# Gated linear attention by pairs of chunks on one Trainium2 core, with ScalarE's Silu on the gate

## What is computed

```python
proj = h @ w_in                       # qa ka va | qb kb vb rb | zb
log_a = log_sigmoid(zb @ w_alpha + b_alpha) / 16
def step(state, (qn, kn, vn, an)):    # four chunks of 64 frames, four heads
    cum = cumsum(an); total = cum[-1]
    k_dec = kn * exp(total - cum)
    state = exp(total) * state + k_dec^T @ vn      # (128, 256) for each head
    return state, qn @ state
ob = rms_norm(o, g_norm_b) * silu(rb)
y = concat([oa, ob]) @ w_out          # then norm, residual, router, experts
```

## Time and profile before

| | us |
|---|---|
| median of 3 runs | 1503.46 |
| lowest and highest | 1501.86, 1504.16 |
| span of the profiled execution, first to last instruction | 1501.0 |

### The profile page before, as it was taken

The page is one execution under the profiler, slowest core; times in us unless marked ns, Lnnn a source line. Parts: engine busy times, 40 slices in busy tenths (PEclk is TensorE's granted clock), DMA queues, the critical chain, the costliest instruction groups (busy, mean ns, idle before and its releaser), DMA issues.

```text
span 1501.0 us, 19016 instructions
## 1 busy us (share of the span) xinstructions
PE 1246.9 (83%) x7349; PEld 552.2 (37%) x7350; DVE 772.2 (51%) x1102; ACT 207.4 (14%) x477; POOL 45.4 (3%) x68
## 2 busy tenths in 40 slices
PE   4699999999999999976777767766776679999977
PEld 4588544744444443322222212212221223333322
DVE  5876257777688666534233323432342334555525
ACT  3011131221111032100000000000000001111103
POOL 0001200000000001000000000000000000000010
PEclk9899999999999999999789898988898989999989
DMA  9999979888789779999999999999999999999996
GB/s 354 393 383 385 368 261 361 307 337 304 295 321 382 306 292 395 427 423 426 428 426 424 428 426 425 425 429 426 425 427 427 426 425 428 426 426 425 427 426 262
DMA packets 101668, 581.93 MB, mean 388 GB/s; under 512 B 6680, under 2 KB 31536, under 8 KB 57856
## 3 DMA queue, kind: packets, MB, share of 16 engines
q1 hardware_dynamic: 98752, 572.81, 93.8%
q10 hardware_dynamic: 1664, 6.46, 1.1%
q0 software_dynamic: 1216, 2.17, 0.5%
HBM read 579.29 MB, written 2.13 MB: 387 GB/s over the span
## 4 chain that ended last, share of the span: by engine, by line
PE 38%; DMA 35%; SPq 16%; DVE 9%; issue 1%; ACT 1%; POOL 0%; ACTq 0%; DVEq 0%
DMA stream<-in_w 32%; PE ps L709 10%; PE ps L918 6%; PE ps L634 5%; SPq L546 5%; SPq L565 4%; SPq L540 4%; PE ps L972 3%; PE ps L791 3%; DMA stream<-in_w_ada 2%; DVE wk L1058 2%; PE ps L879 2%; PE ps L706 1%; PE ps L824 1%; PE ps L925 1%
## 5 line engine op out<-in xcount | busy, mean ns | idle before, releaser
L918 PE MATMUL ps<-stream,wk 128*32 128x512 f32 x2304 | 320.2, 683 | 135.7 <-DMA stream<-in_w 134.9
L1385 DVE TENSOR_TENSOR acc<-ps,acc 128x2048 f32<-128x2048 f32 x37 | 84.8, 2292 | 429.6 <-PE ps L879 429.6
L918 PEld LDWEIGHTS ps<-stream,wk 128*32 128x32 f32 x2304 | 70.6, 117 | 374.4 <-issue 296.6
L972 PE MATMUL ps<-stream,cst 128*32 128x512 f32 x1152 | 153.1, 660 | 61.8 <-DMA stream<-in_w 61.7
L709 PE MATMUL ps<-stream 128*128 128x512 f32 x448 | 199.2, 599 | 0.3 <-PE ps L634 0.3
L709 PEld LDWEIGHTS ps<-stream 128*128 128x128 f32 x448 | 83.9, 191 | 100.3 <-issue 99.6
L634 PE MATMUL ps<-stream 128*128 128x256 f32 x512 | 118.0, 394 | 1.8 <-ACT stream L1530 1.8
L634 PEld LDWEIGHTS ps<-stream 128*128 128x128 f32 x512 | 100.9, 198 | 16.7 <-issue 1.9
L925 PEld LDWEIGHTS ps<-cst,wk 128*128 128x128 f32 x576 | 70.2, 192 | 62.8 <-issue 62.8
L1058 DVE SCALAR_TENSOR_TENSOR wk<-stream,cc,wk 128x768 f32<-128x768 f32 (+1 forms) x90 | 83.6, 929 | 11.5 <-DMA stream<-in_w_ada 8.9
L879 PE MATMUL ps<-wk,cst 32*128 32x512 f32 x592 | 88.3, 668 | 0.8 <-ACT wk L1701 0.8
(11 more groups left out here) (275 smaller groups left out, 1015.5 us busy)
## 6 DMA issues: line engine op xcount, KB each, us to landing
stream<-in_w SPq DMA_DIRECT2D x190, 2048.0 KB, 40.8
stream<-in_w_ada SPq DMA_DIRECT2D x64, 1024.0 KB, 6.0
stream<-in_w_in SPq DMA_DIRECT2D x8, 4096.0 KB, 16.7
stream<-in_w_ada SPq DMA_DIRECT2D x64, 384.0 KB, 10.0
stream<-in_w_out SPq DMA_DIRECT2D x4, 4096.0 KB, 15.3
stream<-in_w_ada SPq DMA_DIRECT2D x16, 512.0 KB, 10.2
stream<-in_w_in SPq DMA_DIRECT2D x4, 2048.0 KB, 13.7
stream<-in_w_in SPq DMA_DIRECT2D x2, 3072.0 KB, 16.2
```

The costliest lines, as they stand in the source:

```text
L918: last = nc.tensor.matmul(bank(1 + m)[32 * g:32 * g + 32, :], xe[:, k + g, :], w13[m][:, k + g, :], start=(k == 0), stop=(k == KD - 4))
L972: last = nc.tensor.matmul(bank(2)[32 * g:32 * g + 32, :], hid[:, k, :], w2v[:, k, 512 * g:512 * g + 512], start=(k == 0), stop=(k == 3))
L1385: V.tensor_tensor(y4, ps[:, b0:b0 + 4, :], y4, ALU.add).then_inc(ysum_sb, 1)
```

## The change

Chunks are worked in pairs. `kv` t now makes both chunks of tile t, head by head: chunk 2t from partitions 0 to 63 and chunk 2t+1 from partitions 64 to 127, into different pairs of banks (`kv_of`). DVE works out both states, in two buffers. `glao` t multiplies both chunks, head by head, into the two halves of the output partitions. `silu` items are gone on both engines: ACT evacuates the blocks of the gate with Silu instead of Copy. The second state buffer takes the place of `la`, which nothing reads any more by then.

```diff
-    for j in range(5):
-        if j:
-            beside[25 + j].append(("glao", j - 1))
-        if j < 4:
-            beside[25 + j].append(("kv", j))
-    beside[26] += [("silu", 0, 0)]
-    beside[28] += [("gsq", 0), ("silu", 1, 0)]
-    beside[29] += [("gmul", 0, 0)]
-    beside[30] += [("gsq", 1), ("silu", 0, 1), ("gmul", 0, 1)]
-    beside[31] += [("gmul", 1, 0), ("glaT", 0)]
+    beside[25].append(("kv", 0))
+    beside[26] += [("glao", 0), ("kv", 1)]
+    beside[27] += [("glao", 1), ("gsq", 0)]
+    beside[28] += [("gsq", 1)]
+    beside[29] += [("gmul", 0, 0), ("gmul", 1, 0)]
+    beside[30] += [("gmul", 0, 1)]
+    beside[31] += [("glaT", 0)]
...
-            out += [("silu", 1, 1), ("gmul", 1, 1), ("partial", 4), ("wout", 0, 0), ("glaT", 1), ("mod", 4)]
+            out += [("gmul", 1, 1), ("partial", 4), ("wout", 0, 0), ("glaT", 1), ("mod", 4)]
...
+        def kv_of(i, h):
+            return bank(6 - 2 * i + h // 2, 2, B_DV)[:, h % 2, :]
...
                     for h in range(B_HEADS):
-                        last = nc.tensor.matmul(bank(6 + h // 2, 2, B_DV)[:, h % 2, :], kdec[lo:lo + CHUNK, t, P * h:P * h + P],
-                                                vb[lo:lo + CHUNK, t, B_DV * h:B_DV * h + B_DV], start=True, stop=True)
+                        for i in range(2):
+                            lo = CHUNK * i
+                            last = nc.tensor.matmul(kv_of(i, h), kdec[lo:lo + CHUNK, t, P * h:P * h + P],
+                                                    vb[lo:lo + CHUNK, t, B_DV * h:B_DV * h + B_DV], start=True, stop=True)
...
-                    pe.wait_ge(state_sb, n + 1)
+                    pe.wait_ge(state_sb, 4 * t + 4)
                     for h in range(B_HEADS):
-                        last = nc.tensor.matmul(bank(2 + 2 * t + h // 2, 2, B_DV)[lo:lo + CHUNK, h % 2, :], qbT[:, h, CHUNK * n:CHUNK * n + CHUNK],
-                                                state[:, h, :], start=True, stop=True)
+                        for i in range(2):
+                            lo, n = CHUNK * i, 2 * t + i
+                            last = nc.tensor.matmul(bank(2 + 2 * t + h // 2, 2, B_DV)[lo:lo + CHUNK, h % 2, :], qbT[:, h, CHUNK * n:CHUNK * n + CHUNK],
+                                                    states[i][:, h, :], start=True, stop=True)
...
+                    for i in range(2):
+                        n = 2 * t + i
+                        if i:
+                            dve.wait_ge(state_sb, 4 * t + 2)
+                        elif t:
+                            dve.wait_ge(gla_ps, 1)
+                        for h in range(B_HEADS):
+                            if n == 0:
+                                ins = V.tensor_copy(states[0][:, h, :], kv_of(0, h))
+                            else:
+                                ins = V.scalar_tensor_tensor(out=states[i][:, h, :], in0=states[1 - i][:, h, :], scalar=st[:, DECAY(n, h):DECAY(n, h) + 1],
+                                                             in1=kv_of(i, h), op0=ALU.mult, op1=ALU.add)
+                        ins.then_inc(state_sb, 2)
...
-                    A(dst, src, ACT.Copy, scale=scale).then_inc(proj_sb, 1)
+                    A(dst, src, ACT.Silu if c >= 10 else ACT.Copy, scale=scale).then_inc(proj_sb, 1)
```

More of the change, by code:

```diff
@@ L255, in build @@
         gl = resid[:, :, :].rearrange("p t d -> p (t d)")
-        kdec, state = view(gl, 0, TT, 512), view(gl, 1024, B_HEADS, B_DV)
+        kdec, states = view(gl, 0, TT, 512), [view(gl, 1024 * (1 + i), B_HEADS, B_DV) for i in range(2)]
         la, tmp = view(gl, 2048, TT, 512), gl[:, 3072:4096]
@@ L395, in build @@
         kv_ps, state_sb, gla_ps = sem("kv_ps"), sem("state_sb"), sem("gla_ps")
-        rb_exp, rb_sb, gla_sq, gla_rs, gla_sb = sem("rb_exp"), sem("rb_sb"), sem("gla_sq"), sem("gla_rs"), sem("gla_sb")
+        gla_sq, gla_rs, gla_sb = sem("gla_sq"), sem("gla_rs"), sem("gla_sb")
         glaT_ps, glaT_sb = sem("glaT_ps"), sem("glaT_sb")
@@ L662, in _ @@
                     if m == 4:
-                        pe.wait_ge(gla_sb, 2)
+                        pe.wait_ge(gla_sb, 3)
                     fold(mod_bank(m)[:, 16 * m:16 * m + 16], 64).then_inc(mod_ps, 1)
@@ L752, in _ @@
                 elif kind == "kv":
-                    n = item[1]
-                    t, lo = n // 2, CHUNK * (n % 2)
-                    if n == 0:
+                    t = item[1]
+                    if t == 0:
                         pe.wait_ge(kdec_sb, 1)
@@ L773, in _ @@
                     t = item[1]
-                    pe.wait_ge(gla_sb, 2 * t + 2)
+                    pe.wait_ge(gla_sb, 3 + t)
                     for j in range(2):
@@ L1261, in _ @@
                                         ALU.mult).then_inc(oT_sb, 1)
[L1262 to L1269, removed]
-                elif kind == "kv":
[L1271 to L1278, removed]
-                                                         op0=ALU.mult, op1=ALU.add)
-                    ins.then_inc(state_sb, 1)
-                    dve.wait_ge(state_sb, n + 1)
+                elif kind == "kv":
+                    t = item[1]
+                    dve.wait_ge(kv_ps, t + 1)
+                    for i in range(2):
[7 more added lines that the diff above has]
+                                ins = V.tensor_copy(states[0][:, h, :], kv_of(0, h))
+                            else:
+                                ins = V.scalar_tensor_tensor(out=states[i][:, h, :], in0=states[1 - i][:, h, :], scalar=st[:, DECAY(n, h):DECAY(n, h) + 1],
+                                                             in1=kv_of(i, h), op0=ALU.mult, op1=ALU.add)
+                        ins.then_inc(state_sb, 2)
                 elif kind == "gmul":
@@ L1284, in _ @@
                     dve.wait_ge(gla_rs, t + 1)
-                    dve.wait_ge(rb_sb, 2 * c + t + 1)
+                    dve.wait_ge(proj_sb, FILLS - 4 + 2 * c + t + 1)
                     for h in (2 * c, 2 * c + 1):
@@ L1619, in _ @@
                         act.wait_ge(o_sq, g + 1)
-                elif kind == "silu":
-                    _, t, c = item
-                    act.wait_ge(proj_sb, FILLS - 4 + 2 * c + t + 1)
-                    act.wait_ge(la_sb, 2)
-                    if c:
-                        act.wait_ge(rb_sb, t + 1)
-                    A(tmp[:, 512 * t:512 * t + 512], rb[:, t, 512 * c:512 * c + 512], ACT.Exp, scale=-1.0).then_inc(rb_exp, 1)
                 elif kind == "gsq":
                     t = item[1]
-                    act.wait_ge(gla_ps, 2 * t + 2)
+                    act.wait_ge(gla_ps, t + 1)
                     act.wait_ge(oT_sb, 4)
```

4 lines of the change are left out of this document (2 added, 2 removed).

## The result

| | before | after |
|---|---|---|
| median, us | 1502.99 | 1493.17 |
| lowest and highest | 1501.86, 1504.16 | 1489.82, 1494.07 |
| runs | 4 | 4 |
| span of the profiled execution | 1501.0 | 1488.0 |

The ratio is 0.993, with a 95% interval of 0.9918 to 0.9942: 9.8 us less, between 8.7 and 12.3. The change makes the kernel faster, by somewhat more than the forecast's 8.65 us; the forecast time was 1494.8 us, in a range of 1491.3 to 1498.2, and 1493.17 lies in it. The profiled execution of after took 1489.82 us, the lowest of its four. Two executions further down, one of before (1802.0 us, granted clock 0.65) and one of the pairs alone (1656.14 us, 0.74), were in a slow state and are left out of every median and ratio.

A forecast was written before the change was run, and what follows sets the result against it. PE was taken to bound the second part and DMA the experts. State products 7.6, the `glaT` 0 wait 0.85 and `mod` 4 0.2 sum to 8.65 us off 1503.46: 1494.8 us, range 1491.3 to 1498.2.

The forecast's parts named there:

- Items of eight at 1.9 us, 7.6 us less: PE's `kv` and `glao`: four items of eight matmuls, each as long as an old item of four; 15.2 us becomes 7.6.
- DVE in time with 3.8 us to spare: DVE's copies and sums for a `kv` pair finish 3.8 us before the `glao` item that needs them.
- Silu and the table loads at nothing: ACT's gate copies with Silu count as equal to Copy; two table loads, slot 25 and before the router's Exp, cost nothing.
- 0.85 us at `glaT` 0, 0.2 at `mod` 4: PE's 0.85 us wait on `gmul` goes; at `mod` 4 ACT's copies limit the gain to 0.2 us (0 to 0.3).
- A shift of one to one: Time saved before `wout` at 463.7 us reaches the kernel's end in full, since expert loads wait on PE's progress.
- The dip stays: The lower granted clock behind PE's wait at `mod` 4, costing 1.7 us, was left in place after the change.
- the rival of 1493.1: The slow clock behind `mod` 4 goes too: 1.7 us more, 10.4 less in all; chance 0.24.
- one wait of 1.80 us with a slow stretch behind it: PE idle of 1.80 us elsewhere, granted clock 0.71 over 353 to 358; used as sign for about 1.9 us behind `mod` 4.
- Shortening one alone brings little: Around the GLA, DVE's and PE's paths are nearly equally long, so only shortening both gains much.
- if DMA became full between 386 and 444 us: Sign that would break the forecast in the GLA; expected 18.0 MB in 50 us, 357 GB/s, under 426.

The follow-up runs named there:

- the pairs alone: The changed kernel with the silu items back on ACT and DVE and a plain copy of the gate; 1500.24 us, ratio 0.9979.
- e1: The changed kernel, but inside an item the four matmuls of one chunk come first, then the four of the other; 1496.12 us, ratio 0.995.
- e4: The changed kernel with Copy instead of Silu on the gate, so no silu and no table loads; 1492.41 us, ratio 0.9923.
- e7: The changed kernel with the copies of the transposes shared, DVE taking the first four blocks and ACT the rest; 1490.57 us, ratio 0.9916.
- e11: Second run of the changed kernel with two unused matmuls of 512 columns on PE behind `mod` 4; 1496.33 us.

## Why the prediction was right, and where it was off

- *Items of eight at 1.9 us, 7.6 us less.* Right: 1.93 and 1.88, four of them 7.62 us instead of 15.17, so 7.55 less. The stretch is shorter by 7.95, because the six slots beside them took 41.85 instead of 42.26 us: five places where items cut into the slots have become three. The sum had no term for that. The Trainium skill's rule on tiles that stood beside this step (TensorEngine Tiling (Array Packing), Key Properties) agrees with 1.9 us, but e1 shows that a change of tile without a drain is not yet an overlap: how much overlaps hangs on the order.
- *DVE in time with 3.8 us to spare.* Right: 3.8 us for the first pair and 3.6 for the second, with 3.34 and 3.04 us of idle ahead of them.
- *Silu and the table loads at nothing.* Right: e4 without them is no faster, and the router's DVE steps, from the one that the first Exp waits for (L1327 before, L1328 after) to the reciprocal, take 3.82 us before and after.
- *0.85 us at `glaT` 0, 0.2 at `mod` 4.* Right in cause, a little small: 1.01 and 0.28, with ACT as the releaser of the second `wout`. Copying faster then moves that end at once (e7).
- *A shift of one to one.* Right: the stretch from the products to the end is the same within 0.4 us.
- *The dip stays.* Wrong, and this is the failed step: "That is nearer to the waits with a dip; I leave the dip where it is". It went, and 1.7 us with it. So it was the rival of 1493.1 that came true, with 1493.17 measured. That the two times agree so well is luck: the traces give 10.94 us against the 10.4 of that rival, and the medians, which wander by a microsecond, 9.8 with an interval that holds both. The other terms were all a little small as well. The prediction had seen one wait of 1.80 us with a slow stretch behind it, and took the length of the wait for the sign. The runs show that the same 1.80 us, elsewhere, have it in some executions and not in others.
- *"Shortening one alone brings little."* Right in number (2.6 and 2.8 of 9.8), but with half the reason. I had DVE's work and PE's as the two paths. The third was the stream of `w_ada` and `w_out`: with its `kv` work done early DVE ran up against slices that stand behind 4 MB of `w_out`, and waited 5 to 10 us for one. The prediction named "if DMA became full between 386 and 444 us" as what would break it. By its mean (349 GB/s over 384 to 434) it was not full, but for 11 us it was, at 405 GB/s. The forecast survived that because DVE had no silu work left around that wait, not because its step had priced it.

## What to carry to other kernels

Two small matmuls that use different halves of the array cost here what one does when they stand next to each other in the queue; write the loop so that halves alternate, not one half after the other. When a stretch is shortened, look at which loads its engines need by its end and what stands ahead of them in the same stream: a mean DMA rate under the limit hid a wait of 10 us for one slice. Two halves of a change can look nearly worthless one by one and still be worth it together, so look in the trace for what takes back the gain of each.

## What was not expected of the hardware

- The same eight matmuls of 256 columns took 1.93 us head by head and 2.89 us chunk by chunk; the second chunk began 0.97 us into the item.
- After waits of the same length the granted clock fell in some executions and not in others: behind 3.15 us at 275.52 and 1.80 at 352.76 not in after's first profile, behind 3.16 and 1.81 in the same places in its second (0.79 both). The first costs 1.68 us each time it comes (78.92 instead of 77.24 us to the next wait), the second nothing, since PE otherwise waits for DVE (31.19 us to `kv` with and without it). What decides it stays open, as does the reason why the 1.80 us behind `mod` 4 never had one.
- A PE wait of 6.64 us in the experts' part (e11), once in fourteen profiled executions, that begins together with nine packets on the `instruction` queue which no other execution has, and a spread of 6 us between the runs of that kernel.
